# Three mixtures of experts on one core: which sums come first at their ends, and a second expert's weights held outside the ring

## The chip, the core and the metric

The kernel runs on one core of one Trainium2 chip. TensorE (PE in the profile) multiplies, VectorE (DVE), ScalarE (ACT) and GpSimd (POOL) do the rest, SyncE (SP) issues nearly all DMAs. The metric is the device time of one launch in microseconds. Three runs of the kernel before took 2087.51, 2088.93 and 2091.18 us; their median, 2088.93 us, is the number to which a time of the changed kernel is compared.

## The reference

All data is float32, for 512 tokens of width 1024. Two layers of a first network follow each other: differential attention, then a mixture of 32 experts; a causal pooling mixer, then a second mixture of 32 experts. A third layer of another kind follows: forgetting attention beside a recurrent unit, then a third mixture. Each mixture takes two experts for each token:

```python
# mixtures 1 and 2 (hidden width 512); token rows are sorted into blocks by expert
h = jax.nn.silu(xb @ w_gate[e]) * (xb @ w_up[e]);  y = h @ w_down[e]
out[token] += y * weight[token, e]
h = layer_norm(DEEPNORM_ALPHA * h + ffn, ln_g, ln_b)      # after mixtures 1 and 2

# mixture 3 (hidden width 256)
hg = silu(t @ w_gate[g]) * (t @ w_up[g]);  y += (hg * combine) @ w_down[g]
return rmsnorm(x + y, final_norm)                         # after mixture 3
```

The code counts mixtures from 0, and so does this text: mixture 0, 1 and 2, `l` in the code.

## The kernel before

**Weights.** Every weight goes through one ring of 12 buffers of 1 MB (`ring`, 128 partitions by 2048 numbers). The queue of SP (`load` inside `mixture`, L517 to L521) waits until TensorE has used the buffer's last content (`units_used`) and issues the next transfer. An expert of mixtures 0 and 1 is six such units, one of mixture 2 three: gate, up, down. The gate and up of the very last expert, number 31, don't go through the ring: `load_spare` (L508) puts them into `hT`, which is free by then, when the ring is full before the mixture begins.

**A slot** is the work for one expert (`slot`, L1011 on TensorE, L1862 on VectorE). TensorE first multiplies the next expert's gate and up (`gate_up`, L992), turns the product of the current one (L899, L900), prepares rows for a pair of experts further on (`ahead`), and multiplies the current down weights (L1035). Rows are prepared in one of two ways. Either TensorE multiplies all tokens by a 0/1 selection (`turn_rows`, L908, 32 matmuls a slot), or, where `gathered_pair` says so, GpSimd has fetched the rows of the pair by an indirect DMA from `x_rows` (`gather_rows`, L2113) and TensorE only transposes them (L956). In mixture 2 pairs 0 to 2 and pair 15, the last, are prepared by selection, pairs 3 to 14 by fetching.

**Results.** ScalarE copies the rows of each pair of experts out, GpSimd stores them to `y_rows` in token order (`store_pair`, L2144). The last pair, experts 30 and 31, isn't waited for: its rows stay in `last_y`, and TensorE multiplies them by a transposed selection with the routing weights in it (`sum_last_pair`, L624) into PSUM banks. In mixtures 0 and 1 that is done for token tiles 0 and 1 of four; the pair's rows of tiles 2 and 3 are stored and loaded as the others. In mixture 2 it is done for all four.

**The end of a mixture.** SP loads each token tile's two result rows back (L584). On VectorE `combine_tile` (L1448) adds one of the two rows, times its weight, to `h`; `add_last` (L1474) adds a PSUM bank of the last pair to `h`; `combine_with_last` (L1462) of mixture 2 does the first row and the bank in one pass, TensorE having added `h` itself into the bank by a product with the identity (L623). `tile_variance` (L1483) and `tile_normal` (L1494, L1498) follow, then TensorE transposes the tile (L690) and multiplies (L643). What sets the order is each engine's own instruction list; the engines meet at semaphores.

## Time and profile before

| | us |
|---|---|
| median of three runs | 2088.93 |
| the profiled execution, as timed | 2091.96 |
| its span, first to last instruction | 2090.1 |
| TensorE busy in the span | 1974.5 |
| VectorE busy in the span | 694.2 |
| ring transfers, GpSimd transfers: MB | 568.06, 27.45 |

The profiled execution is one execution under the hardware profiler, 3.03 us above the median. The profile gives busy time by engine, the span in 40 slices of 52 us, the DMA queues, the chain of work that ended last, and groups of instructions. The trace behind it gives, on request, instructions in order of time, waits, and busy time by window. In the slices mixture 0 lies in 7 to 15, mixture 1 in 19 to 27, mixture 2 in 35 to 38, counted from 1. Within brackets at the end of a row stands how long the engine had been idle before it, and what released it.

### The profile page before, as it was taken

How to read it: one execution, taken by the hardware profiler on the slowest of the kernel's cores; microseconds unless marked ns; L12 is line 12 of the kernel's file. 1: busy time of each engine (PE TensorE's matmuls, PEld its weight loads, DVE VectorE, ACT ScalarE, POOL GpSimd, SP SyncE). 2: the span in 40 equal slices, each digit the busy share in tenths (PEclk: the TensorE clock that was granted, in tenths of full speed). 3: DMA queues.
4: the chain of work that ended last, by engine and by line, in shares of the span. 5: the costliest groups of instructions: out<-in, count | busy, mean ns of one | idle time of the engine just before them, and what ended most of it. 6: DMA issues, size and time to landing. Idle time of an engine off the chain costs nothing.

```text
span 2090.1 us, 25616 instructions
## 1 busy us (share of the span) xinstructions
PE 1974.5 (94%) x10093; PEld 1056.2 (51%) x10093; DVE 694.2 (33%) x1671; ACT 405.0 (19%) x874; POOL 150.7 (7%) x204
## 2 busy tenths in 40 slices
PE   8999989999999998999999999999699999999887
PEld 4444446455554543746554545454544545765454
DVE  0155656311111122635221111111737223532124
ACT  1133432111111111112111111111223222122112
POOL 0111101000000000000100000000010001211100
PEclk9999999999999999999999999999899999999999
DMA  9711105999999998723899999999921111799995
GB/s 335 211 46 47 45 24 181 413 419 421 420 421 421 420 420 354 291 64 103 337 419 419 421 420 421 420 420 408 341 87 40 41 41 44 247 370 419 419 419 209
DMA packets 125874, 596.65 MB, mean 285 GB/s; under 512 B 17287, under 2 KB 44823, under 8 KB 62815
## 3 DMA queue, kind: packets, MB, share of 16 engines
q1 hardware_dynamic: 110559, 568.06, 68.5%
q0 software_dynamic: 15232, 27.45, 4.0%
q8 instruction: 55, 0.90, 0.2%
q14 instruction: 28, 0.23, 0.0%
HBM read 572.95 MB, written 37.01 MB: 292 GB/s over the span
## 4 chain that ended last, share of the span: by engine, by line
PE 81%; DMA 12%; DVE 4%; ACT 2%; issue 1%; SPq 0%; DVEq 0%; ACTq 0%
PE bank L992 22%; PE bank L1035 11%; PE bank L657 10%; PE bank L908 10%; DMA ring<-in_moe_w_up_dram 6%; PE bank L804 5%; DMA ring<-in_w_up_dram 5%; PE bank L671 4%; PE bank L643 3%; PE bank L1166 1%; PE bank L756 1%; PE bank L733 1%; PE bank L899 1%; PE bank L1127 1%; PE bank L720 1%
## 5 line engine op out<-in xcount | busy, mean ns | idle before, releaser
L992 PE MATMUL bank<-ring,work 128*64 128x512 f32 (+1 forms) x3008 | 563.8, 527 | 25.4 <-DMA ring<-in_w_up_dram 20.9
L992 PEld LDWEIGHTS bank<-ring,work 128*64 128x64 f32 x3008 | 225.9, 138 | 359.0 <-issue 330.6
L1035 PE MATMUL bank<-ring,work 128*64 128x512 f32 x1280 | 295.8, 600 | 3.9 <-DVE work L1866 3.9
L1866 DVE COPY work<-bank 128x256 f32<-128x256 f32 (+1 forms) x96 | 36.5, 380 | 691.8 <-PE bank L900 691.8
L908 PE MATMUL bank<-work 128*128 128x128 f32 x2112 | 253.3, 278 | 0.0
L908 PEld LDWEIGHTS bank<-work 128*128 128x128 f32 x2112 | 240.8, 192 | 6.3 <-issue 2.0
L657 PE MATMUL bank<-hT,ring 128*128 128x512 f32 x512 | 234.6, 600 | 0.7 <-ACT work L1229 0.7
L1325 ACT ACTIVATE work<-bank 64x512 f32<-64x512 f32 x96 | 56.7, 591 | 547.1 <-PE bank L1035 544.5
L1035 PEld LDWEIGHTS bank<-ring,work 128*64 128x64 f32 x1280 | 84.3, 136 | 143.9 <-issue 129.0
L657 PEld LDWEIGHTS bank<-hT,ring 128*128 128x128 f32 x512 | 92.6, 191 | 104.9 <-issue 102.9
L1313 ACT ACTIVATE work<-bank 64x512 f32<-64x512 f32 (+1 forms) x96 | 49.8, 518 | 473.2 <-PE bank L992 473.2
L1749 DVE COPY work<-bank 128x512 f32<-128x512 f32 x93 | 64.4, 692 | 231.8 <-PE bank L908 218.1
L2144 POOL DMA_INDIRECT y_rows<-work,y_row x47 | 45.8, 975 | 1058.9 <-ACT work L1326 1002.0
L1756 DVE TENSOR_TENSOR work<-work,bank 64x512 f32<-64x512 f32 (+1 forms) x96 | 88.3, 920 | 18.7 <-ACT work L1313 15.9
L671 PE MATMUL bank<-ring,hT 128*128 128x512 f32 x192 | 86.0, 609 | 0.7 <-DMA ring<-in_attn_w_qkv_dram 0.7
L643 PE MATMUL bank<-hT,ring 128*128 128x128 f32 x512 | 61.4, 282 | 1.5 <-ACT hT L1205 1.5
L643 PEld LDWEIGHTS bank<-hT,ring 128*128 128x128 f32 x512 | 59.9, 198 | 3.4 <-ACT hT L1205 3.4
L899 PEld LDWEIGHTS bank<-con,work 64*128 64x128 f32 x192 | 28.3, 184 | 66.0 <-issue 64.3
L671 PEld LDWEIGHTS bank<-ring,hT 128*128 128x128 f32 x192 | 37.2, 196 | 47.6 <-issue 45.7
L804 PE MATMUL bank<-ring,hT 128*128 128x512 f32 x128 | 57.8, 596 | 1.1 <-ACT hT L1205 1.1
L1326 ACT ACTIVATE work<-bank 64x512 f32<-64x512 f32 x96 | 57.0, 594 | 1.1
L804 PE MATMUL bank<-ring,work 128*128 128x512 f32 x128 | 56.2, 594 | 0.8 <-ACT work L1355 0.8
(308 smaller groups left out, 1676.1 us busy)
## 6 DMA issues: line engine op xcount, KB each, us to landing
ring<-in_moe_w_down_dram SPq DMA_DIRECT2D x128, 1024.0 KB, 16.4
ring<-in_moe_w_gate_dram SPq DMA_DIRECT2D x126, 1024.0 KB, 15.1
ring<-in_moe_w_up_dram SPq DMA_DIRECT2D x126, 1024.0 KB, 17.1
ring<-in_w_down_dram SPq DMA_DIRECT2D x32, 1024.0 KB, 26.0
ring<-in_w_gate_dram SPq DMA_DIRECT2D x31, 1024.0 KB, 22.2
ring<-in_w_up_dram SPq DMA_DIRECT2D x31, 1024.0 KB, 21.9
ring<-in_attn_w_qkv_dram SPq DMA_DIRECT2D x12, 1024.0 KB, 14.9
work<-y_rows SPq DMA_DIRECT2D x12, 1024.0 KB, 7.0
```

What stands on the lines that cost most here:

```text
L643: mm = pe.matmul(bank[2 * i + half][:, P * tt:P * tt + P], v[:, k, P * half:P * half + P], hT[:, k, P * tt:P * tt + P], start=(k == 0), st ...
L657: mm = pe.matmul(banks[:, :], v[:, k, 128 * half:128 * half + 128], hT[:, k, :], start=(k == 0), stop=(k == K - 1))
L671: mm = pe.matmul(banks[tt][:, :], operand[:, 4 * kk + k, P * tt:P * tt + P], v[:, k, :], start=(kk + k == 0), stop=(kk + k == 4))
L804: mm = pe.matmul(bk[:, :], operand(k, tt), v[:, k % 4, :], start=(k == (0 if l else 4)), stop=(k == last))
L908: mm = pe.matmul(XT[half][:, P * k:P * k + width], src[:, tt, c0:c0 + P], sel[buf][:, tt, 0:width], start=(tt == 0), stop=(tt == T - 1))
L992: mm = pe.matmul(GU2[s % 2][BLK * a:BLK * a + BLK, 0:F], xgT[pair % 2][:, per * kk + k, BLK * of_pair:BLK * of_pair + BLK], v[a][:, k, :], ...
L1035: mm = pe.matmul(DN[BLK * n:BLK * n + BLK, :], hT_[:, 2 * kk + k, :], v[:, k, 512 * n:512 * n + 512], start=(kk + k == 0), stop=(2 * kk + ...
L1313: act.activation(sg2[s % 2][:, 0:F], GU2[s % 2][0:BLK, 0:F], ACT.Silu).then_inc(main.sg, 1)
L1325: act.activation(y[rows, 0:512], DN[0:BLK, :], ACT.Copy)
L1326: act.activation(y[rows, 512:D], DN[BLK:P, :], ACT.Copy).then_inc(main.ysb, 1)
L1749: dve.tensor_copy(xgT[buf][:, 4 * half:4 * half + 4, 0:width], XT[half][:, :].rearrange("p (k n) -> p k n", k=4)[:, :, 0:width])\
L1756: dve.tensor_tensor(dealt(hg2[s % 2][:, 0:F], F // P), as_dealt(sg2[s % 2][:, 0:F], F // P), as_dealt(GU2[s % 2][BLK:P, 0:F], F // P), ALU ...
```

## The change

At the ends of mixtures 0 and 1 VectorE's order is turned round and `combine_with_last` is used for tile 1, for which TensorE also adds `h` of tile 1 into the bank. In mixture 2 the gate and up of expert 30 are taken out of the ring too: up goes into `lnp`, where two gain vectors lay, and gate, in eight pieces of 128 KB, into eight places that are free once the routing is done. The second gain vector, `final_norm_2`, is loaded later for that. The last pair of mixture 2 is fetched instead of selected. Helper functions get the mixture as an argument since the number of such experts now depends on it.

```diff
-        def spare_slot(i, s):
-            return type(i) is int and TURN * i + s == E - 1
+        def spare_slot(m, i, s):
+            return spares_to(m, i, s) > 0
+        def spares_to(m, i, s):
+            return max(0, TURN * i + s - E + 1 + len(spare_of[m.l])) if type(i) is int else 0
         def gathered_pair(l, i, c):
             if l == 2:
-                return type(i) is not int or ONE_HOT <= 2 * i + c < E // 2 - 1
+                return type(i) is not int or 2 * i + c >= ONE_HOT
             return False
...
+        spare_of = [range(E - n, E) for n in (1, 1, 2)]
         spare = [hT[:, 4 * a:4 * a + 4, :] for a in range(SPARE)]
+        scraps = [wk(3328, 256), wk(3840, 256), wk(4608, 256), wk(5120, 256), wk(5376, 256), wk(5940, 256),
+                  con[:, C_CAUS:C_CAUS + 256], sm(128, 256)]
...
+        spare_up = lnp.rearrange("p (k n) -> p k n", k=K)
...
+                def load_scraps():
+                    gate, up, _ = list(expert_units(m, l, E - 2))
+                    sp.wait_ge(tiles_written, turns[HEADS[l][1]].src_all)
+                    sp.dma_start(spare_up, up).then_inc(spare_loaded, 16)
+                    sp.wait_ge(routing.ranks, T * (l + 1))
+                    sp.wait_ge(routing.chosen, T * (l + 1))
+                    for k in range(K):
+                        sp.dma_start(scraps[k], gate[:, k, :]).then_inc(spare_loaded, 16)
...
                     if l == 2 and type(i) is int and j == 2:
                         load_spare()
+                        load_scraps()
...
             def sum_last_pair(l, tt, with_rest=False):
+                if with_rest and l < 2:
+                    pe.wait_ge(routing.scaled, T * l + tt + 1)
...
             def project_turned(l, name, src, u0):
                 sum_last_pair(l, 0)
-                sum_last_pair(l, 1)
+                sum_last_pair(l, 1, True)
...
                     for kk in range(m.ng // 2):
                         if 2 * kk < late:
-                            pe.wait_ge(spare_loaded, 16 * SPARE * (l + 1))
-                            v = [spare[a].rearrange("p k n -> p (k n)") for a in range(2)]
+                            if l < 2:
+                                pe.wait_ge(spare_loaded, 16 * SPARE * (l + 1))
+                                v = [[spare[a][:, k, :] for k in range(per)] for a in range(2)]
+                            elif last_slot(i, s):
+                                v = [last_gates, last_ups]
+                            else:
+                                pe.wait_ge(spare_loaded, 16 * SPARE * (l + 1) + 16 * (K + 1))
+                                v = [scraps, [spare_up[:, k, :] for k in range(K)]]
...
             mixture(0)
-            add_last(0, 0)
-            add_last(0, 1)
             combine_tile(0, 0, 0)
             combine_tile(0, 0, 1)
+            add_last(0, 0)
             tile_variance(0)
...
                     if tt == 0:
-                        combine_tile(0, 1, 0)
-                    combine_tile(0, tt + 1, 1)
+                        combine_with_last(0, 1)
+                    else:
+                        combine_tile(0, tt + 1, 1)
                     tile_variance(tt + 1)
...
             mixture(1)        # the same two edits
...
                 for q in range(E // 2 - 1):
                     store_pair(q)
-                    if l == 2 and ONE_HOT + 2 <= q + 4 < E // 2 - 1:
+                    if l == 2 and q == E // 2 - 3:
+                        pool.wait_ge(spare_used, 1)
+                        bcast(lnp[:, D:2 * D], t["final_norm_2"].unsqueeze(0), par.rms12, D)
+                    if l == 2 and ONE_HOT + 2 <= q + 4 < E // 2:
                         pool.wait_ge(main.xt, main.x0 + 2 * (q + 3))
                         gather_rows(q + 4)
...
             bcast(lnp[:, 0:D], t["ffn_norm_2"], par.rms12, D)
-            bcast(lnp[:, D:2 * D], t["final_norm_2"].unsqueeze(0), par.rms12, D)
             router(2, tiles_copied, turns["att2"].copied_all)
```

VectorE's instructions right after mixture 0, before and then changed. L1474 of before and L1502 of the change are `add_last`, L1448 and L1476 `combine_tile`, L1490 `combine_with_last`, L1483 and L1511 the first step of `tile_variance`:

```order
L1474 TENSOR_TENSOR h<-h,bank 128x512 x4
L1448 SCALAR_TENSOR_TENSOR h<-work,h 128x1024 x2
L1483 BN_STATS small<-h 128x6 x2
L1484 BN_AGGR small<-small 128x2
L1487 TENSOR_SCALAR small<-small 128x1
L1492 RECIPROCAL small<-small 128x1
L1494 SCALAR_TENSOR_TENSOR h<-h,small,work 128x1024
L1498 SCALAR_TENSOR_TENSOR h<-h,small,work 128x512 x2
L1448 SCALAR_TENSOR_TENSOR h<-work,h 128x1024 x2
```

```order
L1476 SCALAR_TENSOR_TENSOR h<-work,h 128x1024 x2
L1502 TENSOR_TENSOR h<-h,bank 128x512 x2
L1511 BN_STATS small<-h 128x6 x2
L1512 BN_AGGR small<-small 128x2
L1515 TENSOR_SCALAR small<-small 128x1
L1520 RECIPROCAL small<-small 128x1
L1522 SCALAR_TENSOR_TENSOR h<-h,small,work 128x1024
L1526 SCALAR_TENSOR_TENSOR h<-h,small,work 128x512 x2
L1490 SCALAR_TENSOR_TENSOR h<-work,bank 128x512 x2
L1476 SCALAR_TENSOR_TENSOR h<-work,h 128x1024
```

The two passes over tile 0's fetched rows now stand ahead of the last pair's, and two of the four passes of the last pair are gone; tile 1 gets one pass of two halves more.

TensorE's instructions in the last slots of mixture 2, from the `gate_up` of expert 29 on (L992 and L1021), before and then changed; L908 is a selection, L978 a transposition of fetched rows, L963 and L985 transpose the last selection:

```order
L992 MATMUL bank<-ring,work 64x256 x16
L899 MATMUL bank<-con,work 128x64
L900 MATMUL bank<-con,work 128x64
L908 MATMUL bank<-work 128x128 x16
L1035 MATMUL bank<-ring,work 64x512 x4
L992 MATMUL bank<-ring,work 64x256 x16
L899 MATMUL bank<-con,work 128x64
L900 MATMUL bank<-con,work 128x64
L963 MATMUL bank<-con,work 128x128 x4
```

```order
L1021 MATMUL bank<-ring,work 64x256 x16
L921 MATMUL bank<-con,work 128x64
L922 MATMUL bank<-con,work 128x64
L978 MATMUL bank<-con,work 128x128 x4
L1063 MATMUL bank<-ring,work 64x512 x4
L1021 MATMUL bank<-work 64x256 x12
L1021 MATMUL bank<-con,work 64x256
L1021 MATMUL bank<-work 64x256
L1021 MATMUL bank<-small,work 64x256
L1021 MATMUL bank<-work 64x256
L921 MATMUL bank<-con,work 128x64
L922 MATMUL bank<-con,work 128x64
```

Sixteen matmuls of a selection became four transpositions, here and in the slot before it, and expert 30's sixteen steps read `work`, `con` and `small` in place of the ring.

SP's list where mixture 2's first experts are loaded, of the change; all rows from L531 to L535 are new and stand ahead of the ring's twelfth unit:

```order
L525 DMA hT<-in_w_gate_dram 128x2048
L525 DMA hT<-in_w_up_dram 128x2048
L531 DMA work<-in_w_up_dram 128x2048
L535 DMA work<-in_w_gate_dram 128x256 x6
L535 DMA con<-in_w_gate_dram 128x256
L535 DMA small<-in_w_gate_dram 128x256
L541 DMA ring<-in_w_gate_dram 128x2048
L541 DMA ring<-in_w_up_dram 128x2048
```

Nine transfers moved from the end of the mixture to its beginning, and the next ring load, the twelfth unit, now waits behind them.

## Rows read from the trace of the kernel before

**Rows 1.** The page: GB/s moved by DMA in 40 equal slices.

```profile
GB/s 335 211 46 47 45 24 181 413 419 421 420 421 421 420 420 354 291 64 103 337 419 419 421 420 421 420 420 408 341 87 40 41 41 44 247 370 419 419 419 209
```

**Rows 2.** The page: the chain that ended last, by engine.

```profile
PE 81%; DMA 12%; DVE 4%; ACT 2%; issue 1%; SPq 0%; DVEq 0%; ACTq 0%
```

**Rows 3.** Timeline, mixture 0's end: start us, us, engine, line, instruction, idle before it.

```profile
818.29 0.81 SPq L584 DMA_DIRECT2D work<-y_rows  x2
...
825.79 3.67 PE L624 MATMUL bank<-work 128*128 128x512 f32 x8 [1.38 <-ACT work L1326]
...
827.78 1.41 DVE L1474 TENSOR_TENSOR h<-h,bank 128x512 f32<-128x512 f32 x2 [7.35 <-PE bank L624]
...
833.64 1.42 DVE L1483 BATCH_NORM_STATS2 small<-h 128x6 f32<-128x512 f32 x2
...
838.09 1.97 PE L690 MATMUL bank<-con,h 128*128 128x128 f32 x8 [8.63 <-DVE h L1498]
...
839.89 8.60 PE L643 MATMUL bank<-hT,ring 128*128 128x128 f32 x64
...
845.99 1.41 DVE L1498 SCALAR_TENSOR_TENSOR h<-h,small,work 128x512 f32<-128x512 f32 x2
...
848.33 1.04 PE L690 MATMUL bank<-con,h 128*128 128x128 f32 x8
```

**Rows 4.** One line, L584 in window 818 to 818.6: tile 0's transfer.

```profile
DMA to landing us min/median/max: 4.8/4.8/4.8
```

**Rows 5.** Timeline, mixture 1's end.

```profile
1474.18 1.41 DVE L1474 TENSOR_TENSOR h<-h,bank 128x512 f32<-128x512 f32 x2 [7.35 <-PE bank L624]
...
1480.04 1.42 DVE L1483 BATCH_NORM_STATS2 small<-h 128x6 f32<-128x512 f32 x2
```

**Rows 6.** Windows: us, busy PE, PEld, DVE, ACT, POOL, PEclk, DMA share, GB/s.

```profile
829.00:831.00 2.00, 0.46 (x2) 0.00 (x0) 1.57 (x3) 0.00 (x0) 0.00 (x0) 1.00 1.08 350
...
832.00:833.00 1.00, 0.00 (x0) 0.00 (x0) 0.96 (x2) 0.00 (x0) 0.00 (x0) 0.59 0.08 25
...
1480.00:1482.00 2.00, 0.00 (x0) 0.00 (x0) 1.75 (x5) 0.07 (x1) 0.00 (x0) 0.68 0.84 268
```

**Rows 7.** Timeline, mixture 2's last slots and end.

```profile
2031.14 3.67 PE L992 MATMUL bank<-ring,work 128*64 128x256 f32 x32 [1.86 <-DMA ring<-in_w_up_dram]
...
2035.17 3.84 PE L908 MATMUL bank<-work 128*128 128x128 f32 x32
...
2050.22 3.62 PE L992 MATMUL bank<-ring,work 128*64 128x256 f32 x32
...
2054.20 0.66 PE L963 MATMUL bank<-con,work 128*128 128x128 f32 x4
...
2056.56 3.62 PE L992 MATMUL bank<-hT,work 128*64 128x256 f32 x32
```

**Rows 8.** Timeline, VectorE at mixture 2's end.

```profile
2066.32 2.61 DVE L1448 SCALAR_TENSOR_TENSOR h<-work,h 128x1024 f32<-128x1024 f32 x2 [2.65 <-DMA work<-y_rows]
...
2077.36 1.52 DVE L1462 SCALAR_TENSOR_TENSOR h<-work,bank 128x512 f32<-128x512 f32 x2
```

**Rows 9.** One line, L521 in window 2011.1 to 2011.3: expert 29's gate and up.

```profile
L521 SPq DMA_DIRECT2D ring<-in_w_up_dram x1: 2007/2007/2007, 2011.2 to 2011.2; - x1
...
DMA to landing us min/median/max: 25.1/26.2/27.2
```

**Rows 10.** Windows, as rows 6: mixture 2's beginning, and transfers of 1 KB rows.

```profile
1804.00:1842.00 38.00, 33.76 (x277) 25.77 (x278) 15.39 (x59) 6.88 (x11) 8.21 (x10) 1.00 0.83 280
...
1504.00:1508.00 4.00, 4.00 (x38) 4.00 (x38) 3.79 (x8) 1.65 (x4) 0.00 (x0) 1.00 1.09 348
```

**Rows 11.** Timeline, GpSimd at mixture 2's beginning: the routing table.

```profile
1816.49 0.98 POOL L2129 DMA_INDIRECT slot_token<-small,idx  x1 [0.31 <-issue]
1824.45 0.57 POOL L2135 DMA_DIRECT2D work<-slot_token  x1 [6.97 <-DMA slot_token<-small,idx]
```

**Rows 12.** Timeline, TensorE there, the table's turn.

```profile
1838.51 0.21 PE L969 MATMUL bank<-con,work 32*64 32x32 f32 x1
```

More of the change, by code:

```diff
@@ L403, in program @@
         rms0_gain = wk(3072, D)
+        spare_of = [range(E - n, E) for n in (1, 1, 2)]
         spare = [hT[:, 4 * a:4 * a + 4, :] for a in range(SPARE)]
+        scraps = [wk(3328, 256), wk(3840, 256), wk(4608, 256), wk(5120, 256), wk(5376, 256), wk(5940, 256),
+                  con[:, C_CAUS:C_CAUS + 256], sm(128, 256)]
+        last_gates = [spare[0].rearrange("p a n -> p (a n)").rearrange("p (k n) -> p k n", k=K)[:, k, :] for k in range(K)]
+        last_ups = [spare[1].rearrange("p a n -> p (a n)").rearrange("p (k n) -> p k n", k=K)[:, k, :] for k in range(K)]
+        spare_up = lnp.rearrange("p (k n) -> p k n", k=K)
         xg = [wk(9216 + 2048 * i, D) for i in range(2)]
@@ L527, in slot @@
                         for q, src in enumerate(list(expert_units(m, l, j + 1))[0:m.ng]):
-                            late = SPARE if spare_slot(i, s + 1) else 0
+                            late = SPARE if spare_slot(m, i, s + 1) else 0
                             if q >= late:
@@ L979, in gate_up @@
                     pair, of_pair = s // 2, s % 2
-                    late = SPARE if spare_slot(i, s) else 0
+                    late = SPARE if spare_slot(m, i, s) else 0
                     pe.wait_ge(main.xT, main.x0 + TURN * i + 2 * pair + 2)
@@ L984, in gate_up @@
                         if 2 * kk < late:
-                            pe.wait_ge(spare_loaded, 16 * SPARE * (l + 1))
-                            v = [spare[a].rearrange("p k n -> p (k n)") for a in range(2)]
-                        else:
-                            v = [unit(i, gu_unit(m, i, s) - late + 2 * kk + a) for a in range(2)]
-                        v = [a.rearrange("p (k n) -> p k n", k=per) for a in v]
+                            if l < 2:
[6 more added lines that the diff above has]
+                                v = [scraps, [spare_up[:, k, :] for k in range(K)]]
+                        else:
+                            v = [unit(i, gu_unit(m, i, s) - late + 2 * kk + a).rearrange("p (k n) -> p k n", k=per)
+                                 for a in range(2)]
+                            v = [[a[:, k, :] for k in range(per)] for a in v]
                         for k in range(per):
@@ L993, in gate_up @@
                                                xgT[pair % 2][:, per * kk + k, BLK * of_pair:BLK * of_pair + BLK],
-                                               v[a][:, k, :], start=(kk + k == 0), stop=(per * kk + k == K - 1))
+                                               v[a][k], start=(kk + k == 0), stop=(per * kk + k == K - 1))
                         if 2 * kk >= late:
@@ L1307, in product @@
                 def product(i, s):
-                    if l == 2 and spare_slot(i, s):
-                        act.wait_ge(spare_used, 1)
+                    if l == 2 and spare_slot(m, i, s):
+                        act.wait_ge(spare_used, spares_to(m, i, s))
                     else:
@@ L1453, in combine_tile, with combine_with_last @@
                     link(ins)
-            def combine_with_last(tt):
-                dve.wait_ge(routing.gathered[tt], 16 * 3)
-                dve.wait_ge(last_added, 4 + tt + 1)
+            def combine_with_last(l, tt):
+                dve.wait_ge(routing.gathered[tt], 16 * (l + 1))
+                dve.wait_ge(last_added, 2 * l + tt + 1)
                 for n in range(2):
@@ L1937, in _ @@
             mixture(1)
-            add_last(1, 0)
-            add_last(1, 1)
             combine_tile(1, 0, 0)
             combine_tile(1, 0, 1)
+            add_last(1, 0)
             tile_variance(0)
```

28 lines of the change are left out of this document (14 added, 14 removed).

## The prediction

> **What bounds the kernel now.** I read the page's slices first. Data come in at 413 to 421 GB/s in slices 8 to 15, 21 to 28 and 36 to 39, which are most of the three mixtures; ahead of each mixture the rate falls to 40 to 100 for several slices [rows 1]. So DMA is at a ceiling inside the mixtures and has room ahead of them. Then the chain of waits: 81% of it is TensorE, 12% DMA, 4% VectorE [rows 2]. In order of time the DMA pieces stand in the last third of each mixture only: TensorE eats through what the ring holds ahead, and then waits for gate and up. So a microsecond is worth something (a) on the path after a mixture's last matmul, (b) in a mixture's last slots, and there only as far as neither the stream nor TensorE sets them anyway. The edits sit at just these places, so from here I read timelines.
>
> **Ends of mixtures 0 and 1: the order on VectorE.** TensorE's sum for tiles 0 and 1 starts at 825.79. VectorE has by then waited 7.35 us, and starts `add_last` at 827.78, when tile 0's half of the sum is done. It makes four half passes and two whole ones and reaches tile 0's variance at 833.64 [rows 3]. The fetched rows were there long before: SP issued their transfer at 818.29 and it took 4.8 us [rows 3, 4], so 823.1. In the new order the two whole passes, 2.61 us together by the same instruction in mixture 2 [rows 8], run from about 823.2 to 825.8, inside the old wait. Then `add_last` for tile 0 begins at 827.78 as before and lasts 1.41; variance at 827.78 + 1.41 + 0.06 = 829.25. That is 833.64 - 829.25 = 4.4 us earlier. Mixture 1: add_last at 1474.18, variance at 1480.04 [rows 5]; 1480.04 - (1474.18 + 1.41 + 0.04) = 4.4 us. I assume its fetched rows land as those of mixture 0 do, 4.8 us after their issue, since the last slots of both run alike.
>
> Added: on TensorE two products with the identity for tile 1. The four products there now take 3.67 us [rows 3], 0.9 each, so 1.8 more; TensorE ends at 829.46 + 1.8 = 831.3, and its next work, tile 0's transpositions, can't start before 838.09 - 4.4 = 833.7. Hidden. The wait for `h` scaled by ALPHA has been met since the mixture's head. On VectorE tile 1 costs 1.52 + 1.3 in place of 2.61 [rows 8], 0.2 us, after tile 0's normalisation; TensorE starts tile 1 at 848.33, VectorE has it ready at 845.99 + 1.41 = 847.40 [rows 3], so 0.9 us of cover: nothing.
>
> What is late next is TensorE itself, and here its clock matters. After the sum it sits idle for 8.63 us and its granted clock falls, between 832 and 833, from 2.4 to 1.2 GHz, about 2.9 us after its last matmul; after mixture 1's sum it falls at about 1481, some 5 us after [rows 6]. The 64 matmuls that follow take 8.60 us, part of them at the low clock. With the change the gap in mixture 0 is 831.3 to 833.7, 2.4 us, shorter than either delay, so I expect that the clock stays. Then L690 takes the 1.04 of tile 1's row, not 1.97, and TensorE would be done with tile 0 some 2 us earlier still; but tile 1 is ready only at 847.40 - 4.4 + 0.2 = 843.2. Its last four transpositions then end at 843.8 rather than 849.37: 5.5 us. I take **5.5 for mixture 0** (4.2 if the clock falls) and **4.4 for mixture 1**, where a gap of 10 us remains and the clock will fall as now (4.0 to 4.8).
>
> These 9.9 us reach the end, since nothing before the next mixture runs by itself: DMA idles there, and its stream begins when TensorE frees ring buffers.
>
> **Mixture 2: the last slots.** The last wait for the ring is at 2031.14, for the up of expert 28. From there TensorE works without a gap to 2056.56, expert 31's gate and up: 25.4 us for four slots, two of them with a selection of 3.84, where a fetched pair has 0.66 [rows 7]. A slot with transpositions is 2056.56 - 2050.22 = 6.34 us. Fetching removes 2 x 3.18 = 6.4 us from TensorE. What is late next is expert 29's up: issued at 2011.2, landed 27.2 later, 2038.4 [rows 9]. Today TensorE comes to it at 2031.14 + 6.34 + 3.2 = 2040.7; it would come at 2037.5 and wait. The extra fetch moves 0.5 MB through a full stream, 1.25 us at 420 GB/s [rows 1]. So expert 29 starts at 2038.4 + 1.25 + 0.15 = 2039.8; expert 30, whose gate and up no longer come through the ring, one slot later at 2046.1; expert 31 at 2052.5. Gain 2056.56 - 2052.5 = **4.1 us**. The downs for experts 28 to 31 follow each other in the queue at 2.5 us per MB, from 2042 on, and each is due after 2044: covered. Without the second spare, expert 30's up would land at about 2046, so the spare alone brings little.
>
> Its price lies at the beginning. 2 MB more must go in between 1804 and the time when DMA becomes the limit. From 1804 to 1842 DMA was busy 0.83 of the time [rows 10], that is 6.5 us idle; 2 MB at 420 GB/s are 5.0. Transfers of 1 KB rows ran at 348 GB/s [rows 10], which makes gate 3.0 us rather than 2.5, 5.5 in all. It fits, so I take 0. Bounds: -0.3 (less traffic at the end) and 5.5 (nothing hidden). The nine issues cost SP 0.33 to 0.43 us each, 3.6 us from about 1809, when the last tile's choice is made; SP's next load but one waits until about 1816 for TensorE in any case. The late `final_norm_2` is 0.5 MB in an emptying queue, some 20 us before its first reader; the store behind it on GpSimd waits for expert 29's rows anyway. Its bandwidth may delay the first y rows: VectorE began on them at 2066.32 after a wait, with about 0.7 us in hand [rows 8]. I take 0, bound 1.
>
> The Trainium skill speaks against the eight pieces. Its page "DMA: Bandwidth & Descriptors", section "Bandwidth", advises transfers of at least 1 MB and has 64 KB ones at 138 GB/s. By that the gate would take 7.6 us and 3.6 us would spill out of the 6.5; the sum would be 10.4 instead of 14.0. No row here shows pieces of 128 KB.
>
> **Sum.** 5.5 + 4.4 + 4.1 = 14.0 us. Against the profiled execution: 2091.96 - 14.0 = 2078.0. The median of the runs is 3.03 below that execution, so 2088.93 - 14.0 = **2074.9**.
>
> **Rivals.**
> A. *The spare weights aren't hidden* (0.15): the free DMA time sits in gaps too short or too late, or small pieces waste it. The stream up to expert 29 is 3.6 to 5.5 us later; mixture 2 gives between 0.5 and -1.4. Total 8.5 to 10.4, about 2079.5. Against it: 38 us is long, and TensorE needs nothing from the stream there.
> B. *The ends give half* (0.10): the rows of tiles 2 and 3, whose timing doesn't move, or TensorE's low clock become what tile 1 or 2 waits for. 5.0 + 4.1 = 9.1: 2079.8.
> C. *Mixture 1's stream gives mixture 0's gain back* (0.08), if its DMA time began by itself and not with TensorE. 14.0 - 5.5 = 8.5: 2080.4. Rows 1 speak against it, with 64 and 103 GB/s ahead of it.
> D. *It does not do what it says* (0.04), several of these together, gain below 4.2: about 2087.
> E. *Slower* (0.03): the routing table. Its last scatter is issued at 1816.49, is waited for 6.97 us, and its table is turned on TensorE at 1838.51 [rows 11, 12]. If the table's load takes the 0.6 us of its issue and the 4.8 of rows 4 (an estimate), it is there at 1829.9, 8.6 us early. The spare weights now compete with these scatters of tiny packets. Each microsecond beyond 8.6 stops TensorE; from 8.6 + 14.0 = 22.6 us on the kernel is slower. Four times today's times for both, 3 x 6.97 + 3 x 4.8 = 35.3 us more, would give +12.7: 2101.6. Against it: 2 MB is 5 us of traffic, so a slip beyond 10 is hard to explain.
>
> **How the numbers follow.** The forecast has 0.60: its own range is 2071.5 (clock stays, up of 29 lands as before, 5.3 instead of 4.1, and a run's own scatter) to 2077.5 (clock falls, 1 us lost at the end). A, B and C lie between 2078.5 and 2081. The range 2071 to 2082 holds them all but D, E and the edges. Runs of this kernel differ by 3.7 us, so under 0.2%, 4.2 us, nothing can be told from no change. Faster by over 0.2%: 0.60 + 0.15 + 0.10 + 0.08 = 0.93. Within: 0.04. Slower: 0.03.
>
> **What would show it.** After mixture 0's sum, VectorE: two whole passes before the bank pass, variance about 1.5 us after the first bank pass begins, TensorE's gap about 2.4 us, clock at full, L643's heir of tile 0 at 7.4 us. After mixture 1: gap about 10 us, low clock. In mixture 2: DMA share near 0.97 from 1804 to 1842 (counted in old times), a wait of TensorE for expert 29's up, none for expert 30's, and 12.7 us from the start of expert 29's gate and up to that of expert 31's. It would be wrong if tile 1 or 2 waits for y rows, if TensorE waits for gate and up more than 1.5 us later than now (less the shift of mixtures 0 and 1), or if L969's heir waits.

## The result, and the profile after

The changed kernel takes 2078.47 us (median of 8 runs, 2073.50 to 2083.40), the kernel before 2092.21 beside it (8 runs, 2087.51 to 2095.63). The ratio is 0.9935, with a 95% interval of 0.9921 to 0.9950: 13.6 us less, between 10.5 and 16.5. The forecast was 14.0 less, 2074.9 us. The time itself is 3.6 us above that, and 3.3 of this is the kernel before, whose median rose from 2088.93 (three runs) to 2092.21 (eight): so the two are compared side by side from here on. 2078.47 lies in the range of 2071 to 2082, but outside the forecast's own part of it (2071.5 to 2077.5), just beside that of the rivals A, B and C. The time alone doesn't tell them apart. The profiled execution's span is 2074.0 us, 16.1 under that of before. The ratios below leave out three executions at a low granted clock: two of the kernel before (2332.11 and 3413.75 us, clock 0.84 and 0.55) and one of e3 (2885.66 us, 0.67).

The chain of waits by engine, to be held against [rows 2]: the shares hardly move, since TensorE sets most of the time in both.

```profile
PE 81%; DMA 13%; DVE 3%; ACT 2%; issue 1%; SPq 0%; DVEq 0%; ACTq 0%
```

Mixture 0's end, timeline of the changed kernel (start us, us, engine, line). L1476 adds fetched rows, L1502 the bank, L1511 is the variance; L645 and L646 are the last pair's sum with the stored `h` of tile 1, L712 transposes a tile, L665 multiplies it.

```profile
822.83 2.61 DVE L1476 SCALAR_TENSOR_TENSOR h<-work,h 128x1024 f32<-128x1024 f32 x2 [3.17 <-DMA work<-y_rows]
827.07 1.41 DVE L1502 TENSOR_TENSOR h<-h,bank 128x512 f32<-128x512 f32 x2 [1.63 <-PE bank L646]
828.51 1.43 DVE L1511 BATCH_NORM_STATS2 small<-h 128x6 f32<-128x512 f32 x2
...
825.02 1.96 PE L646 MATMUL bank<-work 128*128 128x512 f32 x4 [1.38 <-ACT work L1354]
...
829.39 1.02 PE L646 MATMUL bank<-work 128*128 128x512 f32 x2
832.96 1.39 PE L712 MATMUL bank<-con,h 128*128 128x128 f32 x8 [2.55 <-DVE h L1526]
834.31 8.92 PE L665 MATMUL bank<-hT,ring 128*128 128x128 f32 x64
...
844.35 7.41 PE L665 MATMUL bank<-hT,ring 128*128 128x128 f32 x64 [0.25 <-ACT hT L1233]
```

The two passes over fetched rows are over at 825.4, inside VectorE's old wait. The variance begins at 828.51, 3.49 us after the start of the sum, where it was 833.64 - 825.79 = 7.85 [rows 3]: 4.36 us, as forecast. TensorE's gap is 2.55 us, forecast 2.4. The products of tile 0 take 8.92 us, not the 7.4 forecast: the clock fell all the same. Windows of the changed kernel, the granted clock is the third number from the right:

```profile
831.00:833.00 2.00, 0.04 (x1) 0.04 (x1) 1.96 (x3) 0.00 (x0) 0.00 (x0) 1.00 0.08 28
833.00:835.00 2.00, 1.99 (x11) 1.49 (x12) 1.93 (x3) 1.19 (x2) 0.00 (x0) 0.77 0.69 233
835.00:837.00 2.00, 2.00 (x11) 2.00 (x11) 1.93 (x3) 0.00 (x0) 0.00 (x0) 0.50 0.99 410
```

The clock is still full in the whole gap, and goes to 1.2 GHz at about 834, when TensorE has been at work again for a microsecond. Tile 1's products begin at 844.35, 19.33 us after the start of the sum. Before it was 23.83:

```profile
849.62 7.41 PE L643 MATMUL bank<-hT,ring 128*128 128x128 f32 x64 [0.25 <-ACT hT L1205]
```

That is 4.5 us, not 5.5.

Mixture 1's end, to be held against [rows 5]: the variance 3.49 us after the sum's start again (7.85), tile 1's products at 1490.52, 25.11 after it. Before it was 29.63, with the sum at 1472.19 and tile 1 at 1501.82 (the rows of the second view). That is 4.5 us.

```profile
1465.41 1.96 PE L646 MATMUL bank<-work 128*128 128x512 f32 x4 [1.38 <-ACT work L1354]
...
1468.90 1.42 DVE L1511 BATCH_NORM_STATS2 small<-h 128x6 f32<-128x512 f32 x2
...
1479.64 1.97 PE L712 MATMUL bank<-con,work 128*128 128x128 f32 x8 [8.85 <-DVE work L1539]
1481.44 7.95 PE L665 MATMUL bank<-hT,ring 128*128 128x128 f32 x64
...
1490.52 7.41 PE L665 MATMUL bank<-hT,ring 128*128 128x128 f32 x64 [0.25 <-ACT hT L1233]
```

```profile
1472.19 3.67 PE L624 MATMUL bank<-work 128*128 128x512 f32 x8 [1.37 <-ACT work L1326]
...
1501.82 7.41 PE L643 MATMUL bank<-hT,ring 128*128 128x128 f32 x64 [0.25 <-ACT hT L1205]
```

Mixture 2's last slots, to be held against [rows 7]: gate and up (L1021) of experts 28 to 31. The first row is the mixture's first gate and up.

```profile
1800.69 3.67 PE L1021 MATMUL bank<-ring,work 128*64 128x256 f32 x32 [0.32 <-ACT work L1320]
...
2020.20 3.67 PE L1021 MATMUL bank<-ring,work 128*64 128x256 f32 x32 [1.84 <-DMA ring<-in_w_up_dram]
...
2027.68 3.67 PE L1021 MATMUL bank<-ring,work 128*64 128x256 f32 x32 [0.93 <-DMA ring<-in_w_up_dram]
...
2034.06 2.76 PE L1021 MATMUL bank<-work 128*64 128x256 f32 x24
...
2040.40 3.62 PE L1021 MATMUL bank<-hT,work 128*64 128x256 f32 x32
```

Expert 29 waits 0.93 us for its up, 30 and 31 wait for nothing. From 28 to 31 it takes 20.20 us, before 25.42. From 29 to 31 it is 12.72, forecast 12.7. The first gate and up of the mixture began at 1800.69, before at 1812.48:

```profile
1812.48 3.67 PE L992 MATMUL bank<-ring,work 128*64 128x256 f32 x32 [0.53 <-DVE work L1749]
```

So expert 28 comes 219.51 us after it, before 218.66. The forecast put 1.25 for the extra fetch into the stream. Whether these 0.85 are its cost this pair of traces doesn't tell, since the same code differs by as much here (below). The mixture gives 25.42 - 20.20 - 0.85 = 4.4 us; 4.1 was forecast.

The spare weights at its beginning, to be held against [rows 10] at the same place (1804 to 1842 of before is 1792 to 1830 here), and the routing table against [rows 11, 12]:

```profile
1792.00:1830.00 38.00, 34.59 (x284) 26.67 (x285) 16.05 (x62) 6.84 (x11) 8.66 (x10) 1.00 0.91 335
```

```profile
1811.29 0.57 POOL L2163 DMA_DIRECT2D work<-slot_token  x1 [6.40 <-DMA slot_token<-small,idx]
```

```profile
1826.72 0.21 PE L991 MATMUL bank<-con,work 32*64 32x32 f32 x1
```

The rate went from 280 to 335 GB/s over 38 us, which is 2.1 MB more: all that was added. The DMA share is 0.91, where about 0.97 was forecast. The scatters are waited for 6.40 us, before 6.97, and the table's turn on TensorE waits for nothing.

### The profile page after: what moved, and what is told of

Its sections match the earlier page's. It is cut to its first block, busy times and chain, and to the rows that moved or that the text cites. A ratio compares the mean times of both kernels' runs of the same rounds, so it can differ in the third digit from the quotient of the medians.

```text
span 2074.0 us, 25525 instructions
## 1 busy us (share of the span) xinstructions
PE 1971.6 (95%) x10045; PEld 1050.5 (51%) x10045; DVE 691.6 (33%) x1669; ACT 404.9 (20%) x874; POOL 151.7 (7%) x205
## 4 chain that ended last, share of the span: by engine, by line
PE 81%; DMA 13%; DVE 3%; ACT 2%; issue 1%; SPq 0%; DVEq 0%; ACTq 0%
PE bank L1021 22%; PE bank L679 10%; PE bank L1063 10%; PE bank L930 10%; DMA ring<-in_w_up_dram 7%; DMA ring<-in_moe_w_up_dram 6%; PE bank L826 5%; PE bank L693 4%; PE bank L665 3%; PE bank L1194 1%; PE bank L778 1%; PE bank L755 1%; PE bank L1155 1%; PE bank L921 1%; PE bank L742 1%; PE bank L712 1%
## 5 line engine op out<-in xcount | busy, mean ns | idle before, releaser
L1021 PE MATMUL bank<-ring,work 128*64 128x512 f32 (+1 forms) x2976 | 559.0, 527 | 28.0 <-DMA ring<-in_w_up_dram 24.2
L1021 PEld LDWEIGHTS bank<-ring,work 128*64 128x64 f32 x2976 | 222.7, 138 | 360.2 <-issue 335.5
L930 PE MATMUL bank<-work 128*128 128x128 f32 x2048 | 245.7, 278 | 0.0
L930 PEld LDWEIGHTS bank<-work 128*128 128x128 f32 x2048 | 233.5, 192 | 6.1 <-issue 2.0
L1784 DVE TENSOR_TENSOR work<-work,bank 64x512 f32<-64x512 f32 (+1 forms) x96 | 88.0, 917 | 19.9 <-ACT work L1341 17.0
L665 PE MATMUL bank<-hT,ring 128*128 128x128 f32 x512 | 61.3, 282 | 1.5 <-ACT hT L1233 1.5
L665 PEld LDWEIGHTS bank<-hT,ring 128*128 128x128 f32 x512 | 59.8, 197 | 3.4 <-ACT hT L1233 3.4
L1233 ACT ACTIVATE hT<-bank 128x512 f32<-128x512 f32 x56 | 31.3, 596 | 134.1 <-PE bank L712 134.0
```

The source lines that it names most:

```text
L665: mm = pe.matmul(bank[2 * i + half][:, P * tt:P * tt + P], v[:, k, P * half:P * half + P], hT[:, k, P * tt:P * tt + P], start=(k == 0), st ...
L930: mm = pe.matmul(XT[half][:, P * k:P * k + width], src[:, tt, c0:c0 + P], sel[buf][:, tt, 0:width], start=(tt == 0), stop=(tt == T - 1))
L1021: mm = pe.matmul(GU2[s % 2][BLK * a:BLK * a + BLK, 0:F], xgT[pair % 2][:, per * kk + k, BLK * of_pair:BLK * of_pair + BLK], v[a][k], start ...
L1784: dve.tensor_tensor(dealt(hg2[s % 2][:, 0:F], F // P), as_dealt(sg2[s % 2][:, 0:F], F // P), as_dealt(GU2[s % 2][BLK:P, 0:F], F // P), ALU ...
```

## The experiments

The runs of one kernel differ by 5 to 14 us, and the sum of mixture 0, up to which all kernels here do the same, starts between 821.39 and 829.88 us in the thirteen traces. So the theories are told apart by four stretches of the one trace that each kernel has, in us. They are: the start of the last pair's sum to tile 1's products in mixtures 0 and 1; the first gate and up of mixture 2 to expert 28's; and expert 28's to expert 31's. The gain is one less the ratio to the kernel before, times 2092 us, with its 95% interval; e1 to e4, e5 to e8 and e9 to e11 each have their own runs of the kernel before beside them.

| kernel | gain | mixture 0 | mixture 1 | to 28 | 28 to 31 |
|---|---|---|---|---|---|
| before | | 23.83 | 29.63 | 218.66 | 25.42 |
| changed | 13.6 (10.5 to 16.5) | 19.33 | 25.11 | 219.51 | 20.20 |
| e1 ends | 7.9 (5.0 to 11.1) | 19.41 | 26.71 | 219.23 | 25.41 |
| e2 mixture 2 | 5.9 (2.1 to 9.6) | 23.35 | 29.63 | 219.72 | 20.19 |
| e3 fetch | 2.9 (0.2 to 5.6) | 24.61 | 29.54 | 219.05 | 22.26 |
| e4 spare | 0.4 (-2.5 to 3.3) | 23.27 | 29.50 | 219.15 | 25.41 |
| e5 order | 6.9 (4.6 to 9.0) | 19.44 | 27.17 | 219.57 | 25.41 |
| e6 fusion | 4.0 (1.0 to 6.7) | 22.72 | 28.62 | 218.83 | 25.41 |
| e7 unused | 2.5 (-0.2 to 5.2) | 23.17 | 29.52 | 219.58 | 22.25 |
| e8 fill | 11.5 (8.8 to 14.2) | 18.24 | 24.47 | 219.25 | 20.19 |
| e9 changed, again | 10.7 (6.9 to 14.2) | 19.05 | 26.14 | 219.53 | 20.19 |
| e10 rows first | 16.5 (11.9 to 21.1) | 18.97 | 23.69 | 220.83 | 20.19 |
| e11 both | 15.5 (11.1 to 19.9) | 18.24 | 22.99 | 220.38 | 20.19 |

What a single trace is worth shows where the code of a stretch is the same. With the old ends mixture 0 takes 23.17 to 24.61 (five traces) and mixture 1 29.50 to 29.63. With mixture 2 as before it is 218.66 to 219.57 to expert 28 (before, e1, e5, e6), a mean of 219.07; with the extra fetch it is 219.05 to 219.72, a mean of 219.44 (e10 and e11, which stand apart, left out). So the fetch costs some 0.4 us, no more than the scatter. The stretch from 28 to 31 repeats within 0.02.

**e1, the ends alone.** Of the change's diff, only `sum_last_pair(l, 1, True)` and the edits behind `mixture(0)` and `mixture(1)`:

```diff
             mixture(0)
-            add_last(0, 0)
-            add_last(0, 1)
             combine_tile(0, 0, 0)
             combine_tile(0, 0, 1)
+            add_last(0, 0)
...
-                        combine_tile(0, 1, 0)
-                    combine_tile(0, tt + 1, 1)
+                        combine_with_last(0, 1)
+                    else:
+                        combine_tile(0, tt + 1, 1)
```

> The kernel before with only the edits at the ends of mixtures 0 and 1. Theory (each term stands by itself): from the start of the last pair's sum to tile 0's variance 3.5 us in place of 7.85 in both mixtures; from it to tile 1's multiplication 19.3 and 25.1 us in place of 23.8 and 29.6. Gain 9.0 us, all of it kept to mixture 2's end: its last slots still follow each other 25.4 us after the last wait for the ring. Rival (mixture 1's stream gives mixture 0's gain back): 4.5 us in all, tile 1 of mixture 1 only 4.5 earlier than before instead of 9.0. Rival (the ends work only together with the edits of mixture 2): under 7 us.

The gain is 7.9. In mixture 0 it is 4.4, in mixture 1 only 2.9. The variance comes 3.5 us after the sum there too, but TensorE needs 9.54 us for tile 0's 64 products, not 7.95:

```profile
1480.61 9.54 PE L644 MATMUL bank<-hT,ring 128*128 128x128 f32 x64
```

Mixture 2's last slots take 25.41, as expected. The rival by which the second mixture gives the first one's gain back falls: from tile 1 of mixture 0 to mixture 1's sum it is 621.24 us, before 622.57. The other rival, under 7, isn't told from the theory by the time, whose interval begins at 5.0; the two stretches give 4.4 + 2.9 = 7.3, short of the 9.0 expected, and what is missing is TensorE's time at the low clock.

**e2, mixture 2's edits alone**: the changed kernel with the ends put back.

```diff
             mixture(0)
+            add_last(0, 0)
+            add_last(0, 1)
             combine_tile(0, 0, 0)
             combine_tile(0, 0, 1)
-            add_last(0, 0)
...
```

> The changed kernel with the ends of mixtures 0 and 1 as before; only mixture 2's edits are in. Theory: 4.1 to 4.4 us faster than before, ratio 0.998; up to mixture 2's first gate and up nothing moves beyond a run's scatter of 1.5 us; from there to expert 28's gate and up 219.5 us in place of 218.7 (0.85 more for the fetched rows' traffic), from expert 28's to expert 31's 20.2 in place of 25.4. Rival (2 us of the 4.4 came from the changed ends, through a stream that starts otherwise): 2.2 us or less.

From mixture 2's first gate and up to expert 31's it is 239.91 us (before 244.08, changed 239.71): 4.2 of mixture 2's gain need nothing of the ends, and the rival's 2.2 falls. The measured 5.9 holds this and 1.7 of scatter, well inside its interval.

**e3, the fetch alone**, one expert outside the ring as before:

```diff
-                return type(i) is not int or ONE_HOT <= 2 * i + c < E // 2 - 1
+                return type(i) is not int or 2 * i + c >= ONE_HOT
```

> The kernel before with only the last pair of mixture 2 fetched instead of selected; expert 30's gate and up still come through the ring. Theory (the ring's last units are the next bound, the second spare takes one wait away): expert 29's gate and up begin 1 us later than in the changed kernel's pattern at most, expert 30's up, 1 MB of gate and 1 MB of up behind expert 29's and its down, lands 7.5 us after expert 29's up, and TensorE, a slot of 6.4 us behind, waits about 1.2 us for it, and again for expert 29's and 30's downs if at all under 1 us. From expert 28's gate and up to expert 31's 21.5 us; 2.9 us faster than before. Rival (the fetch does it all, the spare only fills a place): 4.4 us, no wait at expert 30. Rival (without the spare the stream is 2 MB longer and each later unit 5 us later): 0 us, expert 31 where it was.

```profile
2039.12 3.67 PE L992 MATMUL bank<-ring,work 128*64 128x256 f32 x32 [0.92 <-DMA ring<-in_w_up_dram]
...
2047.53 3.67 PE L992 MATMUL bank<-ring,work 128*64 128x256 f32 x32 [1.85 <-DMA ring<-in_w_up_dram]
```

Expert 30 now waits 1.85 us for its up, where the changed kernel doesn't wait. Gain 2.9 by the runs and 244.08 - 241.31 = 2.8 by the trace, as expected. The wait was named but put at 1.2, and 28 to 31 takes 22.26 for 21.5. The interval of 0.2 to 5.6 alone would leave the rival of 4.4 standing; the wait rules it out.

**e4, the second spare alone**: e2 with the last pair selected again.

```diff
-                return type(i) is not int or 2 * i + c >= ONE_HOT
+                return type(i) is not int or ONE_HOT <= 2 * i + c < E // 2 - 1
```

> Mixture 2 with expert 30's gate and up outside the ring, but the last pair selected by TensorE as before; ends of mixtures 0 and 1 as before. Theory (up to expert 28 the stream is the bound and its length up to there is the same; behind it TensorE works without a wait anyway): 0 us, between -0.5 and +0.5; from expert 28's gate and up to expert 31's 25.4 us as before. Rival (2 MB less late in the mixture shorten the stream by 5 us): 3 to 5 us faster, expert 28's gate and up earlier by that. Rival (the spare weights aren't hidden at the beginning): expert 28's gate and up 3.6 to 5.5 us later, the kernel slower by as much.

```profile
2033.62 3.84 PE L930 MATMUL bank<-work 128*128 128x128 f32 x32
2039.15 3.62 PE L1021 MATMUL bank<-ring,work 128*64 128x256 f32 x32
```

Nothing: 0.4 us (-2.5 to 3.3), and 219.15 and 25.41 us. The two edits of mixture 2 aren't a sum. The spare gives nothing by itself, the fetch 2.8, both 4.2 to 4.4: the spare takes away a wait that only the fetch brings out.

**e5, the order alone**, tile 1 not fused:

```diff
-            add_last(0, 0)
-            add_last(0, 1)
             combine_tile(0, 0, 0)
             combine_tile(0, 0, 1)
+            add_last(0, 0)
...
                     combine_tile(0, tt + 1, 1)
+                    if tt == 0:
+                        add_last(0, 1)
```

> The kernel before with only the order turned round at the ends of mixtures 0 and 1: tile 0's fetched rows first, then its bank, and tile 1's bank after tile 0 is normalised; tile 1 is not fused. Theory: from the start of the sum to tile 0's variance 3.5 us in both mixtures, as in the changed kernel. Tile 1 then costs VectorE 1.41 + 2.61 us where the fused form costs 1.52 + 1.28, so 1.2 more; VectorE is what tile 1 waits for: from the sum to tile 1's multiplication 20.0 us in mixture 0 and 26.3 in mixture 1 (19.3 and 25.1 in the changed kernel, 23.8 and 29.6 before). Gain 7.1 us. Rival (the order alone is everything): 9.0. Rival (the two halves only work together): under 4.

The gain is 6.9, expected 7.1. Mixture 0 was better than expected (19.44), mixture 1 worse (27.17). In mixture 1 tile 0's transpositions read the second normalisation, L1511, and that stands behind tile 1's sums in VectorE's list. I had counted the longer tile 1 for tile 1 only:

```profile
1478.76 2.61 DVE L1448 SCALAR_TENSOR_TENSOR h<-work,h 128x1024 f32<-128x1024 f32 x2
1481.40 1.41 DVE L1474 TENSOR_TENSOR h<-h,bank 128x512 f32<-128x512 f32 x2
1482.84 1.42 DVE L1483 BATCH_NORM_STATS2 small<-h 128x6 f32<-128x512 f32 x2
...
1484.80 1.42 DVE L1511 SCALAR_TENSOR_TENSOR work<-h,small,work 128x512 f32<-128x512 f32 x2
```

**e6, the fusion alone**, tile 0's bank first as before:

```diff
             add_last(0, 0)
-            add_last(0, 1)
             combine_tile(0, 0, 0)
...
-                        combine_tile(0, 1, 0)
-                    combine_tile(0, tt + 1, 1)
+                        combine_with_last(0, 1)
```

> The kernel before with only tile 1 fused (one pass of two halves for its first fetched row and its bank, the stored h added on TensorE) at the ends of mixtures 0 and 1; tile 0's bank still comes ahead of its fetched rows. Theory: VectorE no longer makes tile 1's two bank passes before tile 0's variance, which took 1.41 us and 0.4 of waiting for tile 1's products: from the sum to the variance 6.05 us in place of 7.85, tile 1's multiplication 1.6 us earlier in each mixture. Gain 3.2 us. With the order alone at 7.1 this makes 10.3 where both together give 9.0, since the second pass is taken out of the same place. Rival (tile 1's fusion gives nothing by itself, since TensorE's tile 0 is what tile 1 waits for): under 1 us in mixture 0.

Tile 0's transpositions come 835.59 - 825.06 = 10.5 us after the sum, before 12.3: the 1.8 is there. At tile 1 only 1.1 and 1.0 of it are left, since TensorE takes 9.26 us for the 64 products in place of 8.60 (in mixture 1 8.88 in place of 8.36), being more of its time at the low clock:

```profile
835.59 1.97 PE L691 MATMUL bank<-con,h 128*128 128x128 f32 x8 [5.14 <-DVE h L1499]
837.39 9.26 PE L644 MATMUL bank<-hT,ring 128*128 128x128 f32 x64
```

The time says 4.0 (1.0 to 6.7), the stretches 2.1; the interval holds both. The rival, under 1 us in mixture 0, isn't ruled out: against the mean of the five old ends, 23.65, it is 0.9.

**e7, the spare weights loaded but not used.** The fetch is in, the 2 MB go to their places, expert 30 still comes through the ring:

```diff
-        spare_of = [range(E - n, E) for n in (1, 1, 2)]
+        spare_of = [range(E - n, E) for n in (1, 1, 1)]
...
-                    sp.dma_start(spare_up, up).then_inc(spare_loaded, 16)
+                    sp.dma_start(spare_up, up).then_inc(par.rope, 16)
```

> The kernel before with the last pair of mixture 2 fetched, and the 2 MB of expert 30's gate and up loaded into the places outside the ring at the mixture's beginning as in the changed kernel, but not used: expert 30 still comes through the ring. It has all of the price of the second spare and none of its return. Theory (the 2 MB are hidden in DMA time that idled): the same time as with the fetch alone, 2.8 us under before; from mixture 2's first gate and up to expert 28's 219.1 us, to expert 31's 241.3. Rival (they are hidden only because 2 MB less came at the end, so their price is 5 us and was paid back): to expert 28's 222.7 to 224.6 us, the kernel 1 to 3 us slower than before.

The same stretch of e7 and then of e3, which lacks the 2 MB:

```profile
1804.00:1842.00 38.00, 34.70 (x284) 26.53 (x285) 15.73 (x61) 6.88 (x11) 9.04 (x10) 1.00 0.94 337
```

```profile
1804.00:1842.00 38.00, 34.70 (x284) 26.77 (x285) 16.27 (x64) 6.87 (x11) 9.05 (x10) 1.00 0.82 280
```

57 GB/s more over 38 us are 2.2 MB: the weights lie in DMA time that idled. Expert 28 comes 219.58 us after the first gate and up, 0.5 later than in e3, inside the scatter; the rival wanted 3.6 to 5.5. The gain of 2.5 stands beside 2.9 of e3.

**e8, TensorE's gap filled.** Products into a free bank that nobody reads:

```diff
                 sum_last_pair(l, 1, True)
+                for _ in range((2, 9)[l]):
+                    pe.matmul(bank[2][:, :], ident, last_y[:, 0:512], start=True, stop=True)
```

> The changed kernel with products that nobody reads put into TensorE's gap between the last pair's sum and tile 0's transpositions: 2 in mixture 0, 9 in mixture 1, each 0.9 us. Theory (the low granted clock there costs what TensorE, not VectorE, makes tile 1 wait for): the granted clock stays at 1.00 to tile 1 in both mixtures, tile 0's 64 products take 7.4 us in place of 8.9 and 8.0 to 9.5; from the sum to tile 1's multiplication 18.8 us in place of 19.3 in mixture 0, and 25.1 in mixture 1, as in the changed kernel's profile (26.7 with the ends alone, where the low clock lasted longer). Gain over the changed kernel 0.5 to 1.5 us, too little to be told by the time. Rival (the clock falls whatever TensorE does there): still 0.5 at tile 0's products, 0. Rival (the products delay tile 0's turn): up to 1 us slower.

```profile
831.37 1.88 PE L656 MATMUL bank<-work,con 128*128 128x512 f32 x4
834.08 1.32 PE L714 MATMUL bank<-con,h 128*128 128x128 f32 x8 [0.84 <-DVE h L1528]
835.42 7.41 PE L667 MATMUL bank<-hT,ring 128*128 128x128 f32 x64
```

```profile
833.00:835.00 2.00, 1.16 (x7) 0.67 (x7) 1.93 (x4) 0.23 (x1) 0.00 (x0) 1.00 0.44 67
835.00:837.00 2.00, 1.98 (x18) 1.74 (x17) 1.93 (x3) 0.97 (x2) 0.00 (x0) 1.00 0.86 356
```

The clock stays at 1.00, the 64 products take 7.41, and mixture 0's end takes 18.24 us: 5.6 less than before, the prediction's 5.5 (18.8 was expected of e8). Mixture 1's takes 24.47 (25.1 expected), its 64 products 7.41 too. So the term was right in what a full clock gives, and wrong in that it would stay full. In the time of the whole kernel it doesn't show: 11.5 (8.8 to 14.2), with the changed kernel at 13.6 and 10.7.

**e9 to e11, on one chip.** e9 is the changed kernel again.

> The changed kernel once more, unedited, beside the two that follow, on the same chip. Theory: 13 to 14 us under before, and the granted clock at the ends of mixtures 0 and 1 falls at another moment against TensorE's work than in the first profile, so that from the start of the sum to tile 1's multiplication mixture 0 takes 18.3 to 20.3 us (19.3 in the first profile) and mixture 1 24.5 to 26.7 (25.1). Rival (the moment is fixed by the program): 19.3 and 25.1 again, to 0.1.

19.05 and 26.14, not 19.33 and 25.11: the stretch at the low clock lies otherwise against TensorE's work, and the 64 products of mixture 1's tile 0 take 8.97 us in place of 7.95. Its gain, 10.7, is lower than expected; its interval reaches 14.2.

e10 turns one more order, which e5 had shown: in mixture 1 tile t's second normalisation goes ahead of tile t+1's variance.

```diff
-                    tile_variance(tt + 1)
                 tile_rms(1, tt, rms0_gain, par.rms0, hn, tiles_written)
+                if tt + 1 < T:
+                    tile_variance(tt + 1)
...
                 tile_square(tt)
+                turned("rms0", K, range(tt, tt + 1))
                 if tt + 1 < T:
                     tile_root(rstd, tt + 1)
-                turned("rms0", K, range(tt, tt + 1))
```

> The changed kernel with one more order turned at mixture 1's end: VectorE writes tile t's scaled rows (the second normalisation, from which TensorE's transpositions read) ahead of tile t+1's variance, and ScalarE copies tile t's transposed rows ahead of tile t+1's root. In the changed kernel VectorE has ScalarE's sum of squares of tile 0 from 1475.5 on, and takes it up at 1478.64, after 1.8 us of tile 1's variance. Theory: tile 0's transpositions 12.4 us after the start of the sum in place of 14.2, tile 1's multiplication 23.3 to 24.0 in place of 25.1 to 26.7; 1.2 to 1.8 us under the changed kernel. Rival (ScalarE's copies and roots in the new order hold up tile 1's variance): 0 or up to 1 us slower.

```profile
1471.72 1.28 DVE L1476 SCALAR_TENSOR_TENSOR h<-work,h 128x1024 f32<-128x1024 f32 x1
1473.04 0.17 DVE L1535 RECIPROCAL small<-small 128x1 f32<-128x1 f32 x1
1473.24 1.42 DVE L1539 SCALAR_TENSOR_TENSOR work<-h,small,work 128x512 f32<-128x512 f32 x2
1474.57 1.42 DVE L1511 BATCH_NORM_STATS2 small<-h 128x6 f32<-128x512 f32 x2
```

```profile
1474.05 1.97 PE L712 MATMUL bank<-con,work 128*128 128x128 f32 x8 [7.09 <-DVE work L1539]
1475.85 8.29 PE L665 MATMUL bank<-hT,ring 128*128 128x128 f32 x64
```

Tile 0's transpositions begin 1474.05 - 1461.57 = 12.5 us after the sum (12.4 expected), tile 1's products at 23.69. The median is 2075.05 us (2071.08 to 2079.91, 6 runs) beside 2081.16 of e9: the lowest median here. Its interval against the kernel before, 11.9 to 21.1, still overlaps that of the changed kernel. That it beats the changed kernel is shown in its stretch, by 1.4 to 2.5 us; by the time it is only likely. Two things speak for caution. Of the 7.7 us by which its profiled execution is shorter than e9's (2069.6 and 2077.3), 4.5 lie ahead of mixture 0's sum, where both do the same. And expert 28 comes 220.83 us after mixture 2's first gate and up, some 1.3 later than in the changed kernel. From mixture 1's sum to expert 28 it is 554.3 us, against 554.8 and 557.0 in the changed kernel's two traces: 0.5 to 2.7 us less. What delays expert 28 there is open.

e11 adds the fill, 2 and 7 products.

> The same with products that nobody reads in TensorE's gaps, 2 in mixture 0 and 7 in mixture 1. Theory (the two gains are of different things): granted clock 1.00 up to tile 1 in both; from the sum to tile 1's multiplication 18.2 us in mixture 0 and 22.7 in mixture 1, 3 to 4 us under the changed kernel. Rival (what is saved at mixture 1's end is given back by the clock's fall in the third layer's head, which comes at its own time): 1 to 2 us under it.

The stretches came as expected (18.24; 22.99 for 22.7). The gain of 3 to 4 us over the changed kernel shows only against e9 (4.8), and against e10 there is none: 15.5. The filling is worth 0.7 us in each of the two stretches here and is lost in the scatter. The rival fits as well: from tile 1 of mixture 1 to mixture 2's first gate and up e11 takes 311.88 us, e10 309.75. Of these 2.1 us TensorE loses 0.6 at tile 2, for which it now waits for VectorE's L1541. In the same stretch the clock is low for 17.1 us, in e10 for 13.7; that fits the rest, but no run isolates it.

## Why the prediction was right, and where not

**Mixture 0, 5.5 forecast.** The steps on VectorE and TensorE's gap came within 0.2 us (4.36 for 4.4; 2.55 for 2.4). The step that failed: "the gap in mixture 0 is 831.3 to 833.7, 2.4 us, shorter than either delay, so I expect that the clock stays". It took the fall as something that follows TensorE's last product after a delay. In the eleven traces without filling the fall comes 6.4 to 9.4 us after the start of this sum, with gaps of 2.55 to 8.63 us, and in both traces of the changed kernel after TensorE had resumed. The page "TensorE: Matmul & The Clock Gate" of the Trainium skill (section "Part 1: The HAM clock gate") says that the clock gate's watch on TensorE's activity is free-running and isn't reset when a kernel starts. The traces agree: behind the same sum and the same gap of 2.55 us the fall comes 7.8, 8.1, 9.1 and 9.2 us after the sum's start. Over all traces tile 1 comes 19.2 us after the sum with the changed ends (mean of four) and 23.65 with the old ones (mean of five): 4.5 us. The case "4.2 if the clock falls" stood beside it and was the right one. One pair of traces can give 3.8 to 5.6.

**Mixture 1, 4.4 forecast (4.0 to 4.8).** The first profile gives 4.5, but it was a lucky one: 26.0 is the mean of the three traces with the changed ends, 29.56 of the five with the old ones, so 3.6. The step that failed is the size: "a gap of 10 us remains and the clock will fall as now". With the old order tile 0's transpositions started so late that the low clock took the same of them each time (tile 1 at 29.50 to 29.63 in five traces). Now they start 4.1 us earlier, and what lies at the low clock changes from run to run: 7.95, 8.97 and 9.54 us for the same 64 products. So the term was too high by 0.8 us, and the range of 4.0 to 4.8 lacked the lower cases: e1 gives 2.9.

**Mixture 2, 4.1 forecast.** Right in mechanism and size: 4.4 in the first pair of traces. The mean of six traces with both edits from the first gate and up to expert 31's is 240.1 us, of the four with neither 244.5, and of the one with the spare alone 244.6. Inside the sum two sizes cancel: expert 29's wait was put at 2.3 us (2039.8 - 2037.5) and measured 0.93, and expert 28, which was left at its place, came a little later. The extra fetch, put at 1.25, shows as some 0.4. That the total fits so closely is partly luck. The spare's share was right too ("the spare alone brings little": 0 without the fetch, 1.4 to 1.6 with it), and so was its cost: at most 0.5 us in e7. By the figure that the Trainium skill gives for 64 KB transfers (page "DMA: Bandwidth & Descriptors", section "Bandwidth") an estimated 3.6 us would have spilled over. Here the pieces of 128 KB were issued within 4.1 us and landed 6.8 to 7.7 us after issue in the changed kernel, 8.4 to 9.0 in e7, so several were in flight at once, and they cost nothing that can be seen. The page's figure was taken with transfers issued from GpSimd; these come from SP, and no run here measures one alone.

**The sum.** 4.5 + 3.6 + 4.4 = 12.5 us by the stretches; 13.6 and 10.7 by the two timings of the changed kernel, 14.0 forecast. So the forecast was some 1.5 us high, which its time alone doesn't show. Between the stretches the three traces with the change's ends and nothing else there (changed, e1, e9) take 1.2 us more from tile 1 of mixture 1 to mixture 2's first gate and up than the five with the old ones (311.1 for 309.9), and 1.2 less from tile 1 of mixture 0 to mixture 1's sum (621.3 for 622.5). These cancel. In the first of them the clock is low for 17.1 to 20.5 us, with the old ends for 13.7 in all five, which fits the longer time; what makes them isn't settled beyond that.

**The rivals.** A (spare not hidden) falls with e7 and with the windows. B (the ends give half) named the right cause, TensorE's low clock, but not its size: the ends give 8.0 of 9.9, four fifths. C (mixture 1 gives mixture 0's gain back) falls with e1. D and E don't occur; the routing table was waited for less than before.

## What to carry to other kernels

When two edits sit in one stretch, look what each leaves late: the spare weights were worth nothing until the fetched pair made TensorE early enough to miss them, and the order gave 6.6 us of the ends' 8.0 by itself. Where an engine's list feeds another, put what the other reads ahead of what only this one needs; e10 came of asking which instruction TensorE's wait names. And where a kernel's runs scatter by more than the edit is worth, compare stretches between two of its own landmarks, over several traces: one trace made mixture 1's end look 0.9 us better than the mean of three.

## What the runs showed of the hardware

The granted clock doesn't fall in idle time alone. In the third layer's head TensorE makes 16 products of 8 rows, is busy without a gap, and its clock goes from 2.4 to 1.2 GHz inside this group in all of the thirteen traces. Windows of e1 there:

```profile
1598.00:1600.00 2.00, 2.00 (x6) 0.73 (x5) 1.97 (x4) 0.60 (x1) 0.00 (x0) 1.00 0.00 0
1600.00:1602.00 2.00, 2.00 (x5) 0.82 (x4) 0.71 (x2) 1.26 (x3) 0.00 (x0) 0.79 0.00 0
1602.00:1604.00 2.00, 2.00 (x4) 0.85 (x3) 0.00 (x0) 0.92 (x2) 0.00 (x0) 0.50 0.00 0
```

```profile
1598.54 11.45 PE L1116 MATMUL bank<-work,con 8*128 8x512 f32 x16
```

The same products took 9.80 us in the changed kernel's first profile and 8.71 in e9, the shortest of the thirteen; e1's 11.45 is the longest. The fall comes 2.6 to 5.4 us after their start. So what an edit gains ahead of such a place can shrink or grow in it by up to 2.7 us. Why the clock falls while TensorE is busy no run here isolates.
